# First MLP product begun by halves of the tokens, and the last output projection tiles taken by weight unit

## The reference

```python
y = token_mixer(h, ...)                      # ends in concatenate([fox, gla]) @ w_out
x = x + gate_m * rmsnorm(y, g_post_mix[i])
h = rmsnorm(x, g_pre_mlp[i]) * (1.0 + scale_f) + shift_f
y = squared_relu_mlp(h, w_mlp_in[i], w_mlp_out[i])   # square(relu(h @ w_mlp_in)) @ w_mlp_out
x = x + gate_f * rmsnorm(y, g_post_mlp[i])
```

## Time and profile before

| | us |
|---|---|
| median of three runs | 2250.06 |
| the three runs | 2246.47 to 2250.36 |
| the profiled execution's own time | 2249.3 |
| its span in the trace | 2247.5 |
| PE busy in the span | 2162.5 (96%) |
| DVE busy | 1513.0 (67%) |
| ACT busy | 862.4 (38%) |
| POOL busy | 379.5 (17%) |

### The profile page before, as it was taken

The page is one execution under the profiler, slowest core; times in us unless marked ns, Lnnn a source line. Parts: engine busy times, 40 slices in busy tenths (PEclk is TensorE's granted clock), DMA queues, the critical chain, the costliest instruction groups (busy, mean ns, idle before and its releaser), DMA issues.

```text
span 2247.5 us, 26320 instructions
## 1 busy us (share of the span) xinstructions
PE 2162.5 (96%) x9751; PEld 1765.3 (79%) x9751; DVE 1513.0 (67%) x1460; ACT 862.4 (38%) x1076; POOL 379.5 (17%) x209
## 2 busy tenths in 40 slices
PE   4799999999999998999999999999999999999996
PEld 3578888887777887788888888888878888888885
DVE  6957666666767634665445444544688989898998
ACT  6333333331333224444344335334334444444443
POOL 1000000000000001000000000000034545363645
PEclk9899999999999999999999999999999999999998
DMA  9946654753553342566666646746455664567663
GB/s 366 355 162 217 200 173 146 234 163 115 154 168 136 118 182 75 192 220 225 201 201 220 224 170 205 252 159 201 131 181 180 241 241 161 195 227 244 241 230 145
DMA packets 262305, 441.16 MB, mean 196 GB/s; under 512 B 18156, under 2 KB 110512, under 8 KB 256184
## 3 DMA queue, kind: packets, MB, share of 16 engines
q1 hardware_dynamic: 261376, 435.45, 57.8%
q10 hardware_dynamic: 824, 4.27, 0.5%
HBM read 379.88 MB, written 59.79 MB: 196 GB/s over the span
## 4 chain that ended last, share of the span: by engine, by line
PE 81%; issue 8%; DVE 5%; DMA 2%; POOL 1%; ACT 1%; DVEq 1%; SPq 1%; POOLq 0%; ACTq 0%
PE pair L730 26%; PE pair L732 26%; PE pair L731 25%; DVE am_acc L1750 3%; DMA am_item<-in_w_ada 1%; PE pair L827 1%; PE pair L801 1%; DVE v_op L1978 1%; DVEq L1749 1%; DMA w_raw<-in_w_in 0%; PE pair L818 0%; POOL v_raw L2226 0%; PE pair L1014 0%; PE pair L867 0%; POOLq L2144 0%
## 5 line engine op out<-in xcount | busy, mean ns | idle before, releaser
L730 PE MATMUL pair<-in_hi,w_hi 128*128 128x512 f32 x1792 | 724.0, 404 | 8.1 <-DVE in_lo L1767 6.5
L732 PE MATMUL pair<-in_hi,w_lo 128*128 128x512 f32 x1792 | 702.0, 392 | 0.0
L731 PE MATMUL pair<-in_lo,w_hi 128*128 128x512 f32 x1792 | 701.5, 391 | 0.0
L1510 DVE TENSOR_TENSOR w_lo<-w_raw,w_hi 128x2048 fp32r<-128x2048 f32 (+1 forms) x142 | 292.1, 2057 | 411.8 <-ACT w_hi L1107 411.3
L1107 ACT ACTIVATE w_hi<-w_raw 128x2048 fp32r<-128x2048 f32 (+1 forms) x142 | 244.9, 1724 | 470.6 <-PE pair L732 419.7
L730 PEld LDWEIGHTS pair<-in_hi,w_hi 128*128 128x128 f32 x1792 | 338.6, 189 | 87.5 <-issue 18.9
L732 PEld LDWEIGHTS pair<-in_hi,w_lo 128*128 128x128 f32 x1792 | 338.1, 189 | 73.1
L731 PEld LDWEIGHTS pair<-in_lo,w_hi 128*128 128x128 f32 x1792 | 338.8, 189 | 70.2 <-issue 2.6
L730 PE MATMUL pair<-v_op,hid_r 128*128 128x512 f32 x896 | 349.7, 390 | 5.6 <-DVE y_t L2027 2.2
L732 PE MATMUL pair<-v_op,hid_r 128*128 128x512 f32 x896 | 349.3, 390 | 0.0
L731 PE MATMUL pair<-v_op,hid_r 128*128 128x512 f32 x896 | 349.3, 390 | 0.0
(11 more groups left out here) (204 smaller groups left out, 1881.8 us busy)
## 6 DMA issues: line engine op xcount, KB each, us to landing
w_raw<-in_w_mlp_in SPq DMA_DIRECT2D x64, 1024.0 KB, 5.3
v_raw<-in_w_mlp_out SPq DMA_DIRECT2D x128, 512.0 KB, 5.0
hid_r<-hid_scratch SPq DMA_DIRECT2D x112, 512.0 KB, 6.5
hid_scratch<-hid_r SPq DMA_DIRECT2D x28, 1792.0 KB, 6.5
am_item<-in_w_ada SPq DMA_DIRECT2D x64, 512.0 KB, 7.7
w_raw<-in_w_in SPq DMA_DIRECT2D x128, 256.0 KB, 3.8
af_item<-in_w_ada SPq DMA_DIRECT2D x64, 512.0 KB, 4.6
w_raw<-in_w_in SPq DMA_DIRECT2D x128, 128.0 KB, 3.6
```

The lines of the kernel that those rows point to most:

```text
L730: pe.matmul(dst, a[0], b[0], start=start, stop=False, skip_group_check=onto)
L731: pe.matmul(dst, a[0], b[1], start=False, stop=False, skip_group_check=onto)
L732: return pe.matmul(dst, a[1], b[0], start=False, stop=stop, skip_group_check=onto)
L1510: dve.tensor_tensor(w_lo[n][:, view], w_raw[n][:, view], w_hi[n][:, view].bitcast(F32), ALU.subtract)\
```

## The change

Three things are moved.

The last column group of the output projection took token blocks 2 and 3 one after the other over the second half of k; now it takes both over k 8 to 11, then both over k 12 to 15. The same matmuls, another order.

The first MLP block is cut into 24 pieces. Pieces 0 to 7 are contraction tiles 0 to 7 for the first 256 tokens (rows 0 and 1), pieces 8 to 15 the same tiles for the second 256, pieces 16 to 23 tiles 8 to 15 for all 512. The first 16 pieces take twelve matmuls of 256 columns each instead of 512, so the block has 96 more matmuls and weight loads. A piece has two transposes (pieces 16 to 23: four). The first two pieces are transposed before the product, the others between pieces. Piece 8 is the first that needs all four rows of `y`, and its transposes stand ahead of piece 7's product.

The feeding is reordered. Rows 0 and 1 are finished first; both are scaled on DVE (row 0 was on ACT). Row 2 and row 3 are then finished in between the pieces: each in two half adds on DVE, with pieces 0 to 7 modulated by ACT and weight units 0 and 1 of the MLP split between them. POOL's roots follow that order. ACT issues its four stores of `x_res` after piece 7. From piece 8 on DVE modulates.

```diff
+        PIECES = [(slice(h * HALF, (h + 1) * HALF), k) for h in range(2) for k in range(KT // 2)]
+        PIECES += [(slice(0, SEQ), k) for k in range(KT // 2, KT)]
+        N_PIECES, SECOND = len(PIECES), KT // 2
...
-                    steps += [(k, t) for k0 in (KT // 2, 3 * KT // 4) for t in range(2) for k in range(k0, k0 + KT // 4)]
-                    steps += [(k, t) for t in range(2, TB) for k in range(KT // 2, KT)]
+                    steps += [(k, t) for t0 in (0, 2) for k0 in (KT // 2, 3 * KT // 4) for t in (t0, t0 + 1)
+                              for k in range(k0, k0 + KT // 4)]
...
-            def x1_transpose(k):
-                if k >= 4:
-                    pe.wait_ge(mod_tmp, KT + k - 3)
-                for t in range(TB):
-                    last = pe.transpose(bank[4 + k % 4][:, t * P:t * P + P], y[:, t, k * P:k * P + P], ident[:, :])
+            def x1_transpose(n):
+                cols, k = PIECES[n]
+                if n < 4:
+                    pe.wait_ge(y_mul, (CG - 1) * TB + n + 1)
+                else:
+                    pe.wait_ge(mod_tmp, KT + n - 3)
+                if n == 0:
+                    pe.wait_ge(xn2_dve, 2)
+                if n == SECOND:
+                    pe.wait_ge(xn2_dve, TB)
+                for t in range(cols.start // P, cols.stop // P):
+                    last = pe.transpose(bank[4 + n % 4][:, t * P:t * P + P], y[:, t, k * P:k * P + P], ident[:, :])
                 last.then_inc(x_tr, 1)
-            pe.wait_ge(xn2_ready, 1)
-            pe.wait_ge(xn2_dve, TB - 1)
-            pe.wait_ge(y_mul, CG * TB)
-            for k in range(4):
-                x1_transpose(k)
+            TRANSPOSES_AT = {0: (2,), 1: (3,), 2: (4, 5), 3: (6,), 4: (7,), 6: (8,), 7: (9, 10)}
+            TRANSPOSES_AT.update({n - 3: (n,) for n in range(11, N_PIECES)})
+            for n in range(2):
+                x1_transpose(n)
+            def first_mlp_in():
+                for n, (cols, k) in enumerate(PIECES):
+                    s, m = (k // 4) % 2, M_MLP + k // 4
+                    hi, lo = wide_view(w_hi[s])[:, k % 4, :], wide_view(w_lo[s])[:, k % 4, :]
+                    if k % 4 == 0:
+                        pe.wait_ge(hi_done, m + 1)
+                        pe.wait_ge(lo_done, m + 1)
+                    pe.wait_ge(mod_lo, KT + n + 1)
+                    for t in range(4):
+                        last = split_mm(bank[t][:, cols], (hi[:, t * P:t * P + P], lo[:, t * P:t * P + P]),
+                                        (in_hi[:, k, cols], in_lo[:, k, cols]), k == 0 and n == 0, n == SECOND - 1 or k == KT - 1,
+                                        onto=n >= SECOND)
+                        if k == KT - 1 and t < 3:
+                            last.then_inc(h_sum, 1)
+                        if n >= SECOND and t == 3 and k % 4 == 3:
+                            last.then_inc(w_used, 1)
+                    for following in TRANSPOSES_AT.get(n, ()):
+                        x1_transpose(following)
...
-                    if b == 0 and t == 3 and k + 4 < KT:
-                        x1_transpose(k + 4)
-            for b in range(FBS):
+            first_mlp_in()
+            for b in range(1, FBS):
...
+            def modulate_first(n):
+                cols, k = PIECES[n]
+                act.wait_ge(x_tr, KT + n + 1)
+                act.activation(in_tmp[:, k, cols], bank[4 + n % 4][:, cols], ACT.Identity, scale=mod_a[:, k:k + 1],
+                               bias=mod_b[:, k:k + 1]).then_inc(mod_tmp, 1)
+            def modulated_hi(n):
+                cols, k = PIECES[n]
+                act.wait_ge(mod_tmp, KT + n + 1)
+                act.activation(in_hi[:, k, cols], in_tmp[:, k, cols], ACT.Copy).then_inc(mod_hi, 1)
+            def first_piece(n):
+                modulate_first(n)
+                modulated_hi(n)
             square_y(CG - 1, 0)
             square_y(CG - 1, 1)
-            square_x1(0)
-            act.wait_ge(x1_rstd, 1)
-            act.activation(y[:, 0, :], x_res[:, 0, :], ACT.Copy, scale=rstd[:, 4:5]).then_inc(xn2_ready, 1)
+            square_x1(0, 1)
+            square_x1(1, 2)
+            split_hi_out(CG * MM_O)
             square_y(CG - 1, 2)
-            square_x1(1)
+            first_piece(0)
             square_y(CG - 1, TB - 1)
-            square_x1(2)
-            split_hi_out(CG * MM_O)
-            square_x1(TB - 1, 0)
-            square_x1(TB - 1, 1)
+            first_piece(1)
+            first_piece(2)
             split_hi_out(CG * MM_O + 1)
+            first_piece(3)
+            first_piece(4)
+            square_x1(2, 4)
+            first_piece(5)
+            square_x1(TB - 1, TB + 1, 0)
+            first_piece(6)
+            square_x1(TB - 1, TB + 2, 1)
+            first_piece(7)
             for t in range(TB):
                 act.dma_start(x1_t[:, t, :], x_res[:, t, :]).then_inc(x1_out, 16)
-            for k in range(KT):
-                if k < 2:
-                    act.wait_ge(x_tr, KT + k + 1)
-                    act.activation(in_tmp[:, k, :], bank[4 + k][:, :], ACT.Identity, scale=mod_a[:, k:k + 1],
-                                   bias=mod_b[:, k:k + 1]).then_inc(mod_tmp, 1)
-                act.wait_ge(mod_tmp, KT + k + 1)
-                act.activation(in_hi[:, k, :], in_tmp[:, k, :], ACT.Copy).then_inc(mod_hi, 1)
-                if k in (7, 11):
-                    split_hi_out(CG * MM_O + k // 4 + 1)
+            for n in range(SECOND, N_PIECES):
+                modulated_hi(n)
+                if n in (13, 17):
+                    split_hi_out(CG * MM_O + (n - 5) // 4)
...
-            for t in range(TB):
+            def total_y(t):
                 dve.wait_ge(y_sq, (CG - 1) * TB + t + 1)
                 dve.tensor_reduce(ss4[:, t:t + 1], ss[:, t * CG:(t + 1) * CG], AX_X, ALU.add).then_inc(y_gate, 1)
+            def add_y(t, cols):
+                dve.wait_ge(xres_in[t], 16)
+                dve.wait_ge(y_rstd, t + 1)
+                dve.scalar_tensor_tensor(x_res[:, t, cols], y[:, t, cols], rstd[:, t:t + 1], x_res[:, t, cols],
+                                         ALU.mult, ALU.add).then_inc(x1_ready, 1)
+            def piece_lo(n):
+                cols, k = PIECES[n]
+                dve.wait_ge(mod_hi, KT + n + 1)
+                dve.tensor_tensor(in_lo[:, k, cols], in_tmp[:, k, cols], in_hi[:, k, cols].bitcast(F32),
+                                  ALU.subtract).then_inc(mod_lo, 1)
+            ALL, LEFT, RIGHT = slice(0, D), slice(0, D // 2), slice(D // 2, D)
+            for t in range(2):
+                total_y(t)
                 gain_y(CG - 1, t)
                 dve.drain()
-                dve.wait_ge(xres_in[t], 16)
-                dve.wait_ge(y_rstd, t + 1)
-                for half in range(2 if t == TB - 1 else 1):
-                    cols = slice(half * D // 2, (half + 1) * D // 2) if t == TB - 1 else slice(0, D)
-                    dve.scalar_tensor_tensor(x_res[:, t, cols], y[:, t, cols], rstd[:, t:t + 1], x_res[:, t, cols],
-                                             ALU.mult, ALU.add).then_inc(x1_ready, 1)
-                if t >= 2:
-                    scale_x1(t - 1)
+                add_y(t, ALL)
+            scale_x1(0)
+            scale_x1(1)
+            split_lo(M_MLP, 0)
+            piece_lo(0)
+            total_y(2)
+            gain_y(CG - 1, 2)
+            piece_lo(1)
+            total_y(TB - 1)
+            gain_y(CG - 1, TB - 1)
+            add_y(2, LEFT)
+            piece_lo(2)
+            add_y(2, RIGHT)
+            piece_lo(3)
+            split_lo(M_MLP + 1, 1)
+            piece_lo(4)
+            add_y(TB - 1, LEFT)
+            add_y(TB - 1, RIGHT)
+            piece_lo(5)
+            scale_x1(2)
+            piece_lo(6)
+            piece_lo(7)
             dve.wait_ge(x1_ss, TB + 1)
             dve.tensor_reduce(ss_x[:, TB + 1:TB + 2], ss_x[:, TB - 1:TB + 1], AX_X, ALU.add).then_inc(x1_sq, 1)
             scale_x1(TB - 1)
-            split_lo(M_MLP, 0)
-            for k in range(2):
-                modulated_lo(k, KT + k)
-            for k in range(2, KT):
-                dve.wait_ge(x_tr, KT + k + 1)
-                dve.tensor_scalar(in_tmp[:, k, :], bank[4 + k % 4][:, :], mod_a[:, k:k + 1], mod_b[:, k:k + 1],
+            for n in range(SECOND, N_PIECES):
+                cols, k = PIECES[n]
+                dve.wait_ge(x_tr, KT + n + 1)
+                dve.tensor_scalar(in_tmp[:, k, cols], bank[4 + n % 4][:, cols], mod_a[:, k:k + 1], mod_b[:, k:k + 1],
                                   ALU.mult, ALU.add).then_inc(mod_tmp, 1)
-                if k > 2:
-                    modulated_lo(k - 1, KT + k - 1)
-                if k in (2, 8, 12):
-                    split_lo(M_MLP + max(k // 4, 1), max(k // 4, 1) % 2)
-            modulated_lo(KT - 1, 2 * KT - 1)
+                if n > SECOND:
+                    piece_lo(n - 1)
+                if n in (16, 18):
```

(23 more changed lines are left out.)

## The result

| | before | after |
|---|---|---|
| median of 8 runs each, us | 2248.69 | 2254.87 |
| the runs, us | 2246.36 to 2250.40 | 2253.10 to 2257.68 |
| the profiled execution, us | 2249.3 | 2253.1 |
| its span, us | 2247.5 | 2251.1 |

A forecast was written before the change was run, and what follows sets the result against it. PE, busy 96% of the span, bounds the kernel. Piece 0's 12.5 us gain shrinks to 2.5 at block 0's end, 0.1 at block 1 (ada_times_c); GpSimd's +1.0 makes +0.9: 2250.06 + 0.9 = 2251.0, range 2246.5 to 2257.

The forecast's parts named there:

- The pace of the pieces by DVE: Block 0 until piece 7: DVE's work and waits give four finished rows at 909.6 to 909.7, PE waiting 2.0 us.
- the rival of narrow matmuls that don't halve: Block 0's 256-column matmuls: 0.19 us each instead of 0.12, +8.7 us, 2258.8; at 0.229, +15; chance 0.12.
- Block 0's sum: From 909.7, PE's 40.8 us of work plus feed waits of 0.8 and 1.0 end block 0 at 952.4.
- The weight unit is late next: Ahead of block 1: w_lo behind ada_times_c holds its start to 954.8, PE idle about 2 us.
- If DVE's scale of row 3 starts first: Seam, GpSimd's product with c: it runs until 913.3 and holds lo 8, +1.0; block 1 at 955.8; forecast chance 0.52.
- GpSimd goes first: Seam: GpSimd's product holds row 3's scale 3.6 us, clock adds 1.6; +5.1 us, 2255.2; chance 0.20.
- The feed waits vanish: Block 0: without DVE's 3.3 us of waits and the two later ones, -4.1 us, 2246; partly vanishing has chance 0.13.

The follow-up runs named there:

- pool_after_scale: After, with GpSimd's first product with c waiting until all four rows are scaled: 2251.72 us, ratio to before 1.0011.
- weights_first: After, with ScalarE splitting MLP block 1's first weight unit before its product of w_ada with c: 2249.6 us in one run.
- p7_first: After, with piece 7's matmuls put ahead of piece 8's transposes: ratio to before 1.0019.
- undo_order: After, with the output projection's last column group back in the order of before: 2254.08 us in one run.
- all_three: After, GpSimd's product waiting for block 0's last lo, piece 7 before piece 8's transposes, block 1's first weight split before ada_times_c: 2246.18 us, ratio to before 0.9990.
- before_weights: Before, with block 1's first weight unit split ahead of ScalarE's product of w_ada with c: 2248.3 us in one run.

## Why the prediction was right or wrong

**What the prediction had right.** The range (2246.5 to 2257) holds 2254.87, but by the rival that it took in: the forecast itself was 2251.0, the change +0.9 us where 5.8 was measured, and the mechanism behind it didn't come. Piece 0 was put at 893.0 and came at 893.22. The pace of the pieces by DVE: row 3 scaled at 909.7, against 908.20 + 1.28 in pool_after_scale, 909.9 in after's frame, and PE idle for 2.18 where 2.0 was said. The 256-column spacing is 0.120 us (in piece 0 of after, the second matmul starts at 893.41 and the twelfth at 894.61), which ends the rival of narrow matmuls that don't halve; the narrow lo is 0.42 as put. The 96 more matmuls cost little: at full clock two half pieces take 3.30 us where a tile took 3.20, by that some 0.8 us over the eight tiles (an estimate). Block 0's sum would end at 952.3 (its 2.5 behind piece 7 are the forecast's own) against 952.4. The weight unit is late next by 2.2 to 2.4, as forecast, and weights_first shows that it is ada_times_c ahead of it.

**The step that failed** is in the part on GpSimd, "If DVE's scale of row 3 starts first". It was weighed at 0.52 to 0.20 against "GpSimd goes first", by DVE's 0.04 us behind a root. The product doesn't stand behind a semaphore from the root: it is the next instruction in the same queue, and starts 0.03 before the root's recorded end. The forecast itself subtracted 0.07 of overlap between instructions that follow one another on DVE; used for GpSimd too, that would have made GpSimd first. The trace of before alone didn't settle it: in its one case of a GpSimd instruction right behind a root, with the semaphore long there, that started at 895.79, 0.08 behind the root's end at 895.71. In every trace with DVE's scale and a product that is free to start (after, weights_first, p7_first, undo_order) the product starts 0.06 to 0.07 us ahead of the scale and the scale is 4.62 us: four of four, where the forecast had weighed it as the less likely case. The other condition, that the piece has landed by then, held: it was issued at 892.63.

**The rival was sized well.** It had 5.6 us of idle time (5.52 came), 3.6 for the hold (3.5 at piece 7), 1.6 for the clock (1.9) and block 1 5.1 later (5.1). Its time, 2255.2, stands beside 2254.87, and that is in part luck: it was counted from 2250.06, the median of three runs, where eight gave 2248.69, and the measured change is 5.8 us rather than 5.1. By its row of chances it was one in five.

**A second step was missing.** The clock was charged to the rival alone; the forecast of +0.9 had PE idle for 2.0 us and no price for it. pool_after_scale is that forecast made real, with the scale first, and gives 957.6 at block 1 instead of 955.8. Its ratio is 1.0011 where +0.9 us is 1.0004; the interval, 1.0002 to 1.0020, holds both, so the missing price rests on the timeline. With idle times of 2.18, 2.19 and 2.20 us ahead of the transposes of piece 8 the clock fell in three of three kernels (in pool_after_scale only behind the wait of 1.84 that followed), and in neither of two with 0.76 there and 1.20 ahead of piece 8. The row that could have told it was the earlier trace rows: behind a stretch in which PE was busy 1.21 of 3.40 us it worked at 0.50, and the longest idle time in that stretch was 2.19 us, not 5.6. The forecast took that row for the rival and left it out of its own sum.

**A slip without weight.** In *The feed waits vanish*, 909.7 less 3.3 is 906.4 and not 907, and block 1 would then start at 949.7, not 950.8. The forecast's sum doesn't use it.

**The chances.** Slower by over 0.2% had 0.28, within 0.2% had 0.68. The ratio's middle, 0.26%, is beyond that bound and its lower end, 0.17%, is not.

**Open.** How long the stretch at half clock is differs between executions, 3.4, 6.8 or 10.2 us, without following the idle time ahead of it (5.5 us had 3.4 in weights_first and 6.8 in after). Nor does an idle time of 2.2 us always bring the clock down: ahead of block 1 it did so in none of the seven traces that have that wait. At the seam between the MLP products two waits follow each other some 8 us apart. In four of the twelve traces (after, pool_after_scale, p7_first, undo_order) they are 1.9 and 2.2 us and the clock stays up. In five it falls behind the second, of 2.2. In three (weights_first, all_three, before_weights) it falls within 0.8 us behind the first, of 1.94 to 1.96, and the second is then only 0.6. In weights_first the first wait ends at 1638.42:

```profile
1637.00:1637.50 0.50, 0.00 (x0) 0.00 (x0) 0.41 (x1) 0.50 (x2) 0.00 (x0) 1.00 0.89 262
1638.50:1639.00 0.50, 0.50 (x3) 0.42 (x4) 0.50 (x1) 0.00 (x0) 0.00 (x0) 1.00 0.82 315
1639.50:1640.00 0.50, 0.50 (x3) 0.40 (x2) 0.50 (x1) 0.00 (x0) 0.00 (x0) 0.50 0.02 8
```

What decides it was not found. It moves single profiles by up to some 2 us, so the terms here under 1 us rest on timelines, not on the runs' times.

## What to carry to other kernels

When two engines wait for one event, look which of them gets it through its own queue: here the instruction behind the releasing one started first in four traces of four, and since it was a GpSimd operation of 3.61 us on SBUF, DVE's scale took 3.3 us more. Order them with a wait at a place where the product meets nothing that PE needs soon. A gain of 12 us at the start of a product is only as good as the next supply: count what feeds PE over the whole stretch, fill its waits with work that is ready (piece 7 here stood ready behind a transpose that wasn't), and give the clock a price for each idle stretch that stays.

## What the runs showed of the hardware

- **DVE and GpSimd.** Beside a GpSimd product of 3.61 us, DVE's scale with one SBUF input went from 1.28 to 4.62 us, a lo from 0.42 to 1.42 and a w_lo from 2.29 to 4.89: each ends behind the product, by nearly its own time (1.08, 0.29 and 2.14 us). ScalarE's scale beside it took 2.00. The Trainium skill, SBUF — State Buffer, section Who interferes with whom, says so of DVE operations with two SBUF inputs or in a 2-port mode, the one that starts first holding the other; the traces agree, and show the one-input fp32 scale among them, which no row of before did. Before shows the other direction too: a GpSimd operation of 128x1 that takes 0.19 us elsewhere started inside DVE's two-input add of 883.26 to 885.61 and ended 0.05 us behind it.

```profile
884.23 1.43 POOL L2143 TENSOR_SCALAR ms<-ss_x 128x1 f32<-128x1 f32 x1 [1.07 <-ACT y L1348]
```
- **Starts.** GpSimd's product behind a root in the same queue starts 0.03 us before the root's recorded end (0.03 to 0.04 in five traces); DVE starts 0.04 behind it, so 0.07 decides. One GpSimd instruction of before started 0.08 behind a root's end; why it differs was not found.
- **The narrow matmul.** 256 columns are spaced 0.120 us, 512 columns 0.227, at full clock: half the columns cost 53%. The Trainium skill, TensorE: Matmul & The Clock Gate, section Back-to-back issue gap, gives 262 cycles for a single matmul's gap, which is 0.109 us at 2.4 GHz; the measured value is 10% above it.
- **The clock.** With an idle stretch of 2.2 us and shorter waits on both sides it fell to 0.50 in three kernels of three, in one of them only behind a following wait of 1.84, and in none of seven behind a stretch of 2.2 with PE busy on both sides; with waits of 0.76 and 1.20 it stayed at 1.00. At the seam between the MLP products 1.94 us was enough in three traces of twelve.
